# Gate and up of the two feed-forward stages: two row parts with seven block products instead of eight, and who makes which low part

## The reference

```python
h2 = rms_norm(x, g_norm2) * (1 + sc2) + sh2                       # block 1
x = x + gt2 * ((silu(h2 @ w_gate) * (h2 @ w_up)) @ w_down)        # w_gate, w_up: 2048 x 5632
y = _rms(h, norm_ffn_g)                                            # block 2
h = h + (silu(y @ w_gate_2) * (y @ w_up_2)) @ w_down_2             # w_down: 5632 x 2048
y = _rms(h, norm_ple_g)
h = h + sigmoid(y @ w_ple_gate) * (p @ w_ple_proj)
return _rms(h, final_norm_g)
```

## Time and profile before

| | us |
|---|---|
| median of 3 runs | 2358.84 |
| profiled execution | 2359.86 |
| its span | 2358.1 |
| PE busy | 2298.1 (97%) |
| POOL busy | 1325.7 (56%) |
| ACT busy | 1035.5 (44%) |
| DVE busy | 911.0 (39%) |

### The profile page before, as it was taken

How to read it: one execution, slowest core, us unless ns; L and a number is a source line. 1 busy time by engine, 2 the same in 40 slices (tenths; PEclk the granted TensorE clock), 3 DMA queues, 4 the chain that set the end, 5 groups by cost and what they waited for, 6 DMA issues and landing times.

```text
span 2358.1 us, 29644 instructions
## 1 busy us (share of the span) xinstructions
PE 2298.1 (97%) x10644; PEld 1843.1 (78%) x10644; DVE 911.0 (39%) x1358; ACT 1035.5 (44%) x1285; POOL 1325.7 (56%) x633
## 2 busy tenths in 40 slices
PE   6999988999999999999999999999999999999997
PEld 3577746878888888888888887888888888888886
DVE  4376777870212211112235998511111111111155
ACT  3233464464434444444445444544444444434454
POOL 1101030028888888888882000078888888888840
PEclk9999998999999999999999999999999999999999
DMA  9999895856666656566666565676666566656554
GB/s 384 414 359 370 337 379 207 275 205 190 193 190 192 188 189 193 187 190 192 188 186 222 171 188 161 197 225 194 187 188 194 187 189 193 188 195 188 187 182 148
DMA packets 131563, 518.20 MB, mean 220 GB/s; under 512 B 14497, under 2 KB 20257, under 8 KB 118305
## 3 DMA queue, kind: packets, MB, share of 16 engines
q1 hardware_dynamic: 121552, 449.11, 58.7%
q0 software_dynamic: 9216, 67.11, 7.0%
q10 hardware_dynamic: 720, 0.99, 0.1%
HBM read 512.96 MB, written 4.19 MB: 219 GB/s over the span
## 4 chain that ended last, share of the span: by engine, by line
PE 80%; DVE 2%; ACT 0%; issue 0%; DVEq 0%; ACTq 0%
PE ps L2047 77%; PE ps L1954 1%; PE ps L2016 1%; DVE w_lo L1453 1%; PE ps L2306 0%; DVE fm_lo L1428 0%; PE ps L2258 0%; DVE short L1189 0%; PE ps L1843 0%; PE ps L1865 0%; PE ps L2110 0%; ACT w_hi L704 0%; DVE rstd L1386 0%; ACT fm_hi L724 0%; DVE gate L1721 0%
## 5 line engine op out<-in xcount | busy, mean ns | idle before, releaser
L1035 POOL TENSOR_TENSOR w_lo<-raw,w_hi 128x1024 fp32r<-128x1024 f32 x529 | 1267.9, 2397 | 474.1 <-ACT w_hi L704 474.0
L704 ACT ACTIVATE w_hi<-raw 128x1024 fp32r<-128x1024 f32 x762 | 805.3, 1058 | 1148.8 <-PE ps L2047 1110.1
L2047 PE MATMUL ps<-w_hi,fm_hi 128*128 128x512 f32 x2176 | 854.5, 393 | 2.7 <-DVE w_lo L1453 1.6
L2047 PE MATMUL ps<-w_lo,fm_hi 128*128 128x512 f32 x2176 | 846.6, 389 | 0.0
L2047 PE MATMUL ps<-w_hi,fm_lo 128*128 128x512 f32 x2176 | 846.4, 389 | 0.0
L2047 PEld LDWEIGHTS ps<-w_hi,fm_hi 128*128 128x128 f32 x2176 | 409.6, 188 | 110.7 <-issue 24.5
L2047 PEld LDWEIGHTS ps<-w_lo,fm_hi 128*128 128x128 f32 x2176 | 409.9, 188 | 85.0
L2047 PEld LDWEIGHTS ps<-w_hi,fm_lo 128*128 128x128 f32 x2176 | 410.0, 188 | 81.8
L1453 DVE TENSOR_TENSOR w_lo<-raw,w_hi 128x1024 fp32r<-128x1024 f32 (+1 forms) x233 | 282.3, 1219 | 162.0 <-ACT w_hi L704 158.7
L2047 PE MATMUL ps<-w_hi,hid_hi 128*128 128x512 f32 x640 | 249.2, 389 | 0.0
L2047 PE MATMUL ps<-w_lo,hid_hi 128*128 128x512 f32 x640 | 249.0, 389 | 0.0
(11 more groups left out here) (291 smaller groups left out, 1448.0 us busy)
## 6 DMA issues: line engine op xcount, KB each, us to landing
raw<-in_w_gate SPq DMA_DIRECT2D x176, 512.0 KB, 3.5
raw<-in_w_up SPq DMA_DIRECT2D x176, 512.0 KB, 3.5
raw<-in_w_down SPq DMA_DIRECT2D x176, 512.0 KB, 3.5
ada_raw<-in_w_ada POOLq DMA_DIRECT2D x64, 1024.0 KB, 10.6
raw<-in_w_in SPq DMA_DIRECT2D x120, 512.0 KB, 4.2
raw<-in_w_out SPq DMA_DIRECT2D x64, 512.0 KB, 3.6
ada_raw<-in_w_ada SPq DMA_DIRECT2D x16, 1024.0 KB, 9.7
ada_raw<-in_w_gate SPq DMA_DIRECT2D x16, 1024.0 KB, 4.9
```

What stands on the lines that cost most here:

```text
L704: act.activation(w_hi[:, hi_slot, :, 0:width], raw[:, slot, :, 0:width], ACT.Copy).then_inc(hi_ready, 1)
L1035: pool.tensor_tensor(w_lo[:, slot, :, 0:width], raw[:, slot, :, 0:width], w_hi[:, hi_slot, :, 0:width], ALU.subtract).then_inc(lo_ready, 1)
L2047: last = pe.matmul(banks[t][:, 0:width], a, b, start=kt == 0 and k == 0, stop=kt == kts - 1 and k == 2)
```

## The change

In each of the 10 repeated steps of ffn1 and ffn2, the first four row tiles of gate and up (four pieces: B11, B21 of gate, B12, B22 of up) are no longer four whole pieces, each against both token tiles. The four weight blocks (2 row tiles x 512) and the four operand blocks (2 row tiles x 128 tokens) are multiplied as a 2x2 matrix of blocks with seven products of 6 matmuls instead of eight. The other 12 pieces of gate and up are "conventional" (12 matmuls).

- **DVE, weight sums** (`forms`): U = B11 + B12 into `sum_raw[0]`; V = B12 + B22, in place in B12's raw slot; W = U + B22; Z = W + B21; and the low parts of U, W, Z. ACT makes their `sum_w_hi` and, as before, the hi of every piece, V's too. POOL makes the low parts of all 24 pieces; in front of B11, V, B22 and B21 it waits for the sums that read the raw slot (`form_summed`).
- **DVE, operand sums** once a stage (`mix_operands`): five instructions, the hi on ACT, the low part on DVE; ACT waits for `mixed_raw` ahead of step 0's tanh.
- **Results**: the products go to banks 4 (copied to `sums` by ACT), 5, 6, 7 and 2, 0, 1. `drain_forms` makes from them three sums and adds the rest of gate and up to them later (`gate_sums`, `up_sums`); silu and hidden read `sums` in SBUF. PE waits for `drained` ahead of the transposes, which now stand after conventional piece 4.
- **ffn1's down** is added to `ungated` (set to zero before step 0), and multiplied by gate2 and added to x in the last step (`settle`, eight instructions of 128x1024).
- **w_hi** has six tiles in the feed-forward stages; the sixth lies at 100 KB. So `final_g` is loaded after the last piece of ffn2 is used, in SP's order ahead of ple_g's loads.
- **gate2**: 5 pieces behind heads, 11 in out1, one for every two weight pieces. `emb` and `result` have other places.

```diff
+FFN_HI = 6
+CONVENTIONAL = [(part, j) for part in (0, 1) for j in range(2, UP)]
+STEP_ORDER = [("c", 0), ("b11", 0), ("c", 1), ("sum_u", 0), ("sum_v", 0), ("b22", 0), ("c", 2), ("sum_w", 0), ("b21", 0), ("c", 3),
+              ("sum_z", 0)] + [("c", k) for k in range(4, len(CONVENTIONAL))]
+TURN_AFTER = ("c", 4)
...
@@ SP
-                sp.dma_start(final_g[:, :], bass.AP(io["final_norm_g_2"].tensor, 0, [[0, P], [1, D]])).then_inc(final_landed, 16)
             sp_ffn(sp, piece, "ffn2", io["w_gate_2"], io["w_up_2"], io["w_down_2"], before_ffn2)
+            sp.wait_ge(pieces_used, FIRST["ffn2"] + FFN_PIECES)
+            sp.dma_start(final_g[:, :], bass.AP(io["final_norm_g_2"].tensor, 0, [[0, P], [1, D]])).then_inc(final_landed, 16)
             units("ple_g", io["w_ple_gate_2"], range(4))
...
@@ ACT
+            def forms(i):
+                split_body(i, a, 24, (M_C0, M_B11))
+                sum_hi(i, 0, 1)
+                split_body(i, a, 24, (M_C1,))
+                act.wait_ge(form_summed, i * 4 + 4 * before + 2)
+                split_body(i, a, 24, (M_V, M_B22, M_C2))
+                act.wait_ge(pieces_used, i * 24 + a + M_B11 + 1)
+                act.wait_ge(hidden_ready, i + done + 1)
+                act.activation(sums[:, 0, :], ps[:, 4, :], ACT.Copy).then_inc(sum_copied, 1)
+                sum_hi(i, 1, 3)
+                split_body(i, a, 24, (M_B21, M_C3))
+                sum_hi(i, 2, 4)
...
@@ POOL
+                for m, sums_needed in ((M_C0, 0), (M_B11, 1), (M_V, 2), (M_B22, 3), (M_B21, 4)):
+                    if sums_needed:
+                        pool.wait_ge(form_summed, i * 4 + 4 * before + sums_needed)
+                    rest_loop(i, a, 24, {M_C0: (M_C0,), M_B11: (M_B11, M_C1), M_V: (M_V,), M_B22: (M_B22, M_C2), M_B21: range(M_B21, 24)}[m])
...
@@ DVE
+            def silu(i):
+                dve.wait_ge(tanh_done, i + done + 2)
+                dve.scalar_tensor_tensor(silu_t[:, :, :], silu_t[:, :, :], 1.0, sums[:, 0:2, :], ALU.add, ALU.mult).then_inc(silu_step, 1)
+            def drain_forms(i):
+                dve.wait_ge(form_used, i * 3 + 3 * before + 3)
+                dve.wait_ge(sum_copied, i + before + 1)
+                dve.tensor_tensor(sums[:, 1, :], ps[:, 7, :], sums[:, 0, :], ALU.add).then_inc(drain_step, 1)
+                dve.wait_ge(drain_step, i * 2 + 2 * before + 1)
+                dve.tensor_tensor(sums[:, 2, :], ps[:, 5, :], sums[:, 1, :], ALU.subtract).then_inc(drain_step, 1)
+                dve.wait_ge(drain_step, i * 2 + 2 * before + 2)
+                dve.tensor_tensor(sums[:, 1, :], sums[:, 1, :], ps[:, 6, :], ALU.add)
+                dve.tensor_tensor(sums[:, 3, :], sums[:, 2, :], ps[:, 6, :], ALU.subtract).then_inc(drained, 1)
+            def forms(i, adds=None):
+                if adds:
+                    adds(2)
+                dve.wait_ge(form_used, i * 3 + 3 * before + 1)
+                landed(i, M_B11)
+                landed(i, M_V)
+                dve.tensor_tensor(sum_raw[0][:, :, :], piece_raw(M_B11), piece_raw(M_V), ALU.add).then_inc(form_summed, 1)
+                if adds:
+                    adds(3)
+                landed(i, M_B22)
+                dve.tensor_tensor(piece_raw(M_V), piece_raw(M_V), piece_raw(M_B22), ALU.add).then_inc(form_summed, 1)
+                summed(i, 1)
+                dve.tensor_tensor(sum_raw[1][:, :, :], sum_raw[0][:, :, :], piece_raw(M_B22), ALU.add).then_inc(form_summed, 1)
+                sum_low(i, 0)
+                landed(i, M_B21)
+                summed(i, 3)
+                dve.tensor_tensor(sum_raw[2][:, :, :], sum_raw[1][:, :, :], piece_raw(M_B21), ALU.add).then_inc(form_summed, 1)
+                sum_low(i, 1)
+                summed(i, 4)
+                sum_low(i, 2)
+            def settle(d):
+                cols = slice(d * NW, (d + 1) * NW)
+                dve.wait_ge(down_read, LEAD + (FFN_STEPS - 2) * 4 + d + 1)
+                link(dve.tensor_tensor(ungated[:, :, cols], ungated[:, :, cols], gate2[:, cols].unsqueeze(1).to_broadcast([P, TT, NW]), ALU.mult))
+                link(dve.tensor_tensor(x[:, :, cols], x[:, :, cols], ungated[:, :, cols], ALU.add))
+            def step_body(i):
+                drain_forms(i)
+                hidden_lo(i + done + 1)
+                gate_sums(i)
+                silu(i)
+                up_sums(i)
+                add_step(i, 0)
+                add_step(i, 1)
+            mix_operands()
+            if not done:
+                dve.wait_ge(emb_spilled, 16)
+                link(dve.memset(ungated[:, :, :], 0.0))
+            silu_first()
+            forms(0)
+            with dve.Fori(0, FFN_STEPS - 2) as i:
+                step_body(i)
+                forms(i + 1, lambda d: add_step(i, d))
...
@@ PE
+            def gate_up(i):
+                pe.wait_ge(gate_read, i + done + 1)
+                for kind, k in STEP_ORDER:
+                    m = STEP_PIECES.index((kind, k)) if (kind, k) in STEP_PIECES else None
+                    if kind == "c":
+                        conventional(i, m, k)
+                    elif kind == "b11":
+                        pe.wait_ge(down_read, LEAD + i * 4 + 4 * done - 1)
+                        low_wait(i, m)
+                        form(4, plain(0, 0), lambda e: piece_tiles(m, e), True, True).then_inc(pieces_used, 1)
+                    elif kind == "sum_u":
+                        sum_wait(i, 0)
+                        form(5, mixture(1), sum_tiles(0), True, True).then_inc(form_used, 1)
...
+                    if (kind, k) == TURN_AFTER:
+                        pe.wait_ge(drained, i + before + 1)
+                        turn_hidden(i + done + 1)
+                pe.wait_ge(hid_lo_ready, i + done + 1)
```

## The result

The changed kernel takes 2481.68 us (median of 4 runs, 2480.24 to 2484.66), the kernel before 2358.44 (4 runs, 2358.02 to 2359.76): a ratio of 1.0524, 95% interval 1.0512 to 1.0536. Forecast were 2488. The profiled execution of the changed kernel ran 2480.24 us with a span of 2478.5, against 2359.86 and 2358.1 before: +120.4 of span. By the medians it is +123.2; the profiled execution before is slower than any of the four times above, the profiled one after is the fastest of its four, so the spans differ by somewhat less.

What follows compares the result with a forecast made beforehand. PE was taken to bound the kernel (busy 2298.1 of 2358.1 us). Terms 98.6 + 6.3 + 3.4 + 9.6 + 10.9 = +128.8 on 2358.8 gave 2488 us; range 2390 to 2535.

Steps and rivals of the forecast that it cites:

- The bound and what goes: FFN steps: PE paces at 66.2 us; 186 matmuls instead of 192 would let PE alone run 64.8.
- The shared path and its price: FFN steps: DVE instructions with two SBUF inputs take turns with POOL's, each costing POOL 0.98 us, from a row of 2.85.
- The bounds 0.45 and 1.22: POOL's loss per DVE instruction, lowest and highest: 67.9 us a step (+35) or 72.5 (+127).
- The schedule of a step: Repeated FFN steps: C3's low part ends at 22.13, PE begins c3 5.96 late; 71.10 us a step, +98.6 over 20.
- Step 4: In each FFN step, after sum_z: PE waits for four linked DVE reads of PSUM, 0.33 us more.
- First form step: First form step of each FFN: sum 0 stands behind step 0's `hidden`, 3.15 us more, twice: +6.3 (0 to 8).
- mix_operands: FFN 1's start: five SBUF instructions beside POOL delay piece 11, +3.4 us (0 to 8); FFN 2: 0.
- settle: End of FFN 1: eight SBUF instructions delay add_last, for which PE's third down product waits: +9.6 us (0 to 14).
- End of FFN 2: Before ple_g: final_g's load goes ahead of ple_g's pieces in SP's order, so PE starts late: +10.9 us (6 to 14).
- The 1.5 us added for piece 1: Start of ple_g: ACT has two squares and four fm_hi before piece 1, 1.5 us more.
- Heads and out1: Three gate2 pieces move: heads -3 to -6 us, out1 +1 to +6; taken as 0 (-5 to +4).
- Clock: PE's clock in the form stretch, between two observed busy levels: 0 (up to +34 us); rival that it falls, 2522, chance 0.06.

Runs made afterwards that it cites:

- e3: Changed kernel, but DVE makes seven pieces' low parts each step and POOL starts its pieces only after DVE's three sum lows: 2361.21 us.
- e7: Changed kernel with the edits of e3, e4 and e5 together: 2340.27 us, ratio 0.9919 to the kernel before.
- e5: Changed kernel, but the last step's down products add `ungated` in PSUM, without settle's eight SBUF instructions: 2469.00 us.
- e4: Changed kernel, but final_g's load is issued behind ple_g's first six pieces: 2471.68 us.
- e6: Kernel before, with only the new gate2 order (three of eight pieces leave the heads for out1): 2356.62 us, ratio 0.9994.
- e2: Changed kernel plus one more DVE instruction with both inputs in SBUF ahead of each of the three low parts: 2542.71 us.

## Why the prediction was right

**The bound and what goes (right).** PE alone paces at 64.8: e3 and e7 step at 64.8, with 2.2 us of waits in all 20 steps.

**The shared path and its price (right).** The earlier trace rows were the whole case, and the rows of after look like them: 3.4 for DVE, 3.35 for POOL. The price read as 0.98 from one row of 2.85 was 0.95. The bounds 0.45 and 1.22 were honest but far apart; the row taken was the good one. The Trainium skill, "SBUF — State Buffer", section "Who interferes with whom", has the rule from which a full 1.22 would follow, and also that a DVE instruction with at most one SBUF input does not contend: the memset at 0.91 and the PSUM adds at 0.686 agree with the second; for the first, POOL's rows show 0.95 lost, less than the whole 1.22.

**The schedule of a step (right, with one wrong line).** C3's low part was forecast 22.13 after the start of the step; it ended at 22.18 (with a start 0.3 later and turns a little shorter than forecast). PE's waits stand before c1, sum_u, c2 and c3 as listed. Step 4 is wrong: the four linked reads (926.13 to 928.87) run before sum_z and PE never waits for them. They wait for a count of 3 in `form_used`, which starts at 1, so the product with W (`sum_w`) releases them, and they read banks 5 to 7, which are complete by then. Without the 0.33 the forecast is 70.77 a step, measured 70.90.

**First form step (right in size, wrong in kind).** 3.15 an FFN was forecast as waiting; the steps are 2.7 (FFN 1) and 2.9 (FFN 2) longer than the others. In FFN 1 PE's waits of that step are 3.08, 0.38, 0.94 and 1.65; with 0.3 for each restart 7.25, against 6.1 of a usual step: +1.2. In FFN 2 they are 5.1 in three waits, 6.0 with restarts: nothing more than usual. The late sum 0 takes the place of the other waits instead of standing on top of them. The rest, 1.5 and 2.9, is clock, which fell behind the first long wait. FFN 2 (length; PE, PEld, DVE, ACT, POOL busy; PEclk; DMA; GB/s):
```profile
1636.38:1643.21 6.83, 6.04 (x15) 4.17 (x15) 6.83 (x3) 4.53 (x6) 6.83 (x3) 0.50 0.23 77
```

**mix_operands (near; FFN 2 overlooked).** FFN 1: 3.4 forecast, 2.56 of idle and 0.3 of restart. FFN 2 was put at 0 because POOL would not be at work yet. It was: its first low part of the stage starts at 1598.81, and the first two operand sums (1603.02 and 1606.47) take 3.42 and 2.50 beside it. ACT stood behind them until 1610.30 and PE waited 0.98, 1.3 us with the restart.

**settle (right place, the sum made up of more).** 9.6 forecast, 12.8 measured: PE's hole was 7.4, 7.7 with its restart. The rows of DVE alternate as written, but two of the four multiplications took 2.10. Not forecast were the 2.4 us of POOL's late low parts ahead of the hole and the 2.6 of clock behind it (e5).

**End of FFN 2 (right).** From one turn of x to the next 17.31 us where it was 6.33: +10.98, forecast 10.9. e4 gave 10.0 back. The chain in the trace of after, start and duration:
```profile
2366.55 0.33 SPq L444 DMA_DIRECT2D final_g<-in_final_norm_g  x1
2366.92 2.90 SPq L490 DMA_DIRECT2D raw<-in_w_ple_gate  x6
```
```profile
2372.38 1.06 ACT L799 ACTIVATE w_hi<-raw 128x1024 fp32r<-128x1024 f32 x1 [15.57 <-DMA raw<-in_w_ple_gate]
```
```profile
2376.01 0.77 PE L2355 MATMUL ps<-w_hi,fm_hi 128*128 128x512 f32 x1 [8.62 <-POOL w_lo L1136]
```
SP's issue 0.2 after T = 2366.35, the split at T + 6.0 (forecast 6.5), PE at T + 9.7 (forecast 10.2). The 1.5 us added for piece 1 were wrong in kind: PE waits once, and the rest is clock (4.0 us of work in a slice of 0.51; the matmuls show 2.1 lost). So the 10.9 is partly luck: 8.8 for the hole and 2.1 of clock, where 9.4 and 1.5 were added up.

**Heads and out1 (mis-sized, the largest miss).** Taken as 0 with bounds of -5 and +4; the profiled execution shows -8.3 and +0.6. By the list behind e6 about half of the -8.3 goes with the clock of that execution, and e6's timed runs show no gain that can be told.

**Clock (mis-sized).** Taken as 0, from two windows of the heads between which the form stretch was to lie. Within the usual steps that held: the waits are split into pieces of 0.9 to 1.4, and windows of the steps stand at 1.00. Behind longer waits it did not: 1.5 and 2.9 us in the two first form steps, 2.6 behind settle, 2.1 at ple_g, 9 us in all.

The terms, forecast and as the trace of after shows them (us):

| | forecast | measured |
|---|---|---|
| 20 steps | 98.6 | 94.4 |
| first form steps | 6.3 | 5.6 |
| step 0, FFN 1 and FFN 2 | 3.4 and 0 | 2.9 and 1.3 |
| settle | 9.6 | 12.8 |
| end of FFN 2 | 10.9 | 10.9 |
| heads and out1 | 0 | -7.7 |
| sum | 128.8 | 120.2 (the span: 120.4) |

The range held because the one large term was read from rows of the same two engines doing the same thing. That the other terms add up so nearly is partly luck: time put down to waits was clock in three places, and misses of both signs cancel.

## What to carry to other kernels

Before work is given to the idler of VectorE and GpSimd, look for a row in which both work with two SBUF operands: there VectorE's busy share says little, since its instructions stretch to GpSimd's length and GpSimd's grow too. Keep the two apart in time, or let VectorE take the whole burst; in e3 that needed more VectorE instructions and less VectorE time. Price a hole in TensorE with the clock behind its end (a window that holds the hole too counts clock that nobody used), and give back the small moves at the borders (a load's place in a queue, a loop of adds) before judging a change of the arithmetic: here two of them were worth 10.0 and 12.7 us, the arithmetic 27. When an experiment's total comes out as forecast, compare the rows as well: in e2 and e5 the number was right and the account wrong.

## What the runs showed of the hardware

- A 128x1024 VectorE subtraction with both inputs in SBUF takes 1.22 us alone and up to 3.4 beside a subtracting GpSimd, whose 2.40 becomes 3.35; a memset of 128x1024 (0.91) and adds with one PSUM input (0.686) don't change.
- The cost of a wait of TensorE is more than its idle time: per step of after 4.8 us of idle made 6.1 of delay, four waits, so 0.3 each. Of the 0.3, 0.16 is the last row before the wait, 0.39 long where the next start would come after 0.227; behind the wait the first matmuls start 0.33 and 0.24 apart.
- TensorE's granted clock fell to its lower level (0.50) around one hole of 4.66 us in e2's steps, and the 4.7 us of work behind it ran at 0.43 us a matmul instead of 0.227; it did not fall after four of 0.9 to 1.4 us in a stretch of after's steps (1.00).
- In the heads the same code ran at a granted clock between 0.57 and 1.00 in eight kernels that differ only elsewhere.
